# Even attention of a two-block network: a step's four scores in two banks, steps in pairs, masks first, one group copied by VectorE

## The reference

```python
z = h @ w_in
q_a, c_kv, q_i, k_i, w_i, q_b, k_b, v_b = jnp.split(z, ...)
o_a = dsa_attention(...)     # 8 heads; each query attends to the 64 keys that an index score selects
o_b = diff_attention(...)    # 4 heads, each a difference of two softmaxes: p[:, :, 0] - lam * p[:, :, 1]
return jnp.concatenate([o_a, o_b], axis=-1) @ w_out
```

## Time and profile before

| what | value |
|---|---|
| median of 3 runs | 1346.38 us (1346.29 to 1346.5) |
| the profiled execution: its own time | 1346.09 us |
| its span in the trace | 1344.2 us |
| PE busy | 99% of the span |
| DVE, ACT, POOL busy | 72%, 55%, 9% |
| mean granted clock of TensorE | 0.999 of full |
| the even attention, first score to first product of the output projection | 788.61 to 816.57 us |

### The profile page before, as it was taken

How to read it: one execution, slowest core, us unless ns; L and a number is a source line. 1 busy time by engine, 2 the same in 40 slices (tenths; PEclk the granted TensorE clock), 3 DMA queues, 4 the chain that set the end, 5 groups by cost and what they waited for, 6 DMA issues and landing times.

```text
span 1344.2 us, 19217 instructions
## 1 busy us (share of the span) xinstructions
PE 1334.3 (99%) x7365; PEld 1121.7 (83%) x7365; DVE 974.3 (72%) x1502; ACT 740.2 (55%) x1155; POOL 125.3 (9%) x114
## 2 busy tenths in 40 slices
PE   9999999999999999999999999999999999999998
PEld 6888888888888888888888777888888878888886
DVE  7566878777664767877778687886667887786665
ACT  6564555554545754555445676754445675654443
POOL 1000011111000000311111002220000010400000
PEclk9999999999999999999999999999999999999999
DMA  9743545555455334656655524357765524355552
GB/s 375 246 153 129 187 158 193 187 195 192 173 219 186 127 126 160 228 200 231 202 189 201 170 95 151 117 216 227 216 204 193 182 79 173 119 206 193 191 191 88
DMA packets 37673, 244.32 MB, mean 182 GB/s; under 512 B 4656, under 2 KB 5312, under 8 KB 10192
## 3 DMA queue, kind: packets, MB, share of 16 engines
q1 hardware_dynamic: 33568, 228.08, 47.9%
q0 software_dynamic: 3728, 14.82, 3.9%
q10 hardware_dynamic: 288, 0.21, 0.1%
HBM read 241.13 MB, written 1.97 MB: 181 GB/s over the span
## 4 chain that ended last, share of the span: by engine, by line
PE 97%; DVE 1%; ACT 1%; DMA 0%; issue 0%; POOL 0%; ACTq 0%; DVEq 0%
PE ps L1217 19%; PE ps L1155 17%; PE ps L1161 16%; PE ps L1164 16%; PE ps L1224 10%; PE ps L1323 3%; PE ps L1418 2%; PE ps L1449 2%; PE ps L1400 1%; PE ps L2034 1%; PE ps L1265 1%; PE ps L1259 1%; PE ps L1262 1%; PE ps L1577 1%; PE ps L2044 1%; PE ps L1578 1%
## 5 line engine op out<-in xcount | busy, mean ns | idle before, releaser
L2736 DVE TENSOR_TENSOR wlo<-raw,whi 128x1024 fp32r<-128x1024 f32 (+2 forms) x423 | 510.4, 1217 | 264.2 <-ACT whi L2151 263.1
L2151 ACT CAST whi<-raw 128x1024 fp32r<-128x1024 f32 (+1 forms) x431 | 444.6, 1041 | 332.9 <-PE ps L1224 188.5
L1217 PE MATMUL ps<-act,whi 128*128 128x512 f32 x1120 | 266.4, 390 | 0.0
L1217 PEld LDWEIGHTS ps<-act,whi 128*128 128x128 f32 x1120 | 208.4, 188 | 42.2
L1155 PE MATMUL ps<-whi,mhi 128*128 128x512 f32 (+2 forms) x688 | 235.7, 392 | 0.3 <-DVE mlo L2760 0.3
L1161 PE MATMUL ps<-wlo,mhi 128*128 128x512 f32 (+2 forms) x688 | 231.1, 385 | 0.0
L1164 PE MATMUL ps<-whi,mlo 128*128 128x512 f32 (+2 forms) x688 | 231.0, 385 | 0.0
L1164 PEld LDWEIGHTS ps<-whi,mlo 128*128 128x128 f32 x688 | 129.2, 188 | 26.4
L1161 PEld LDWEIGHTS ps<-wlo,mhi 128*128 128x128 f32 x688 | 129.2, 188 | 26.1 <-DVE wlo L2736 0.5
L1224 PEld LDWEIGHTS ps<-act,wlo 128*128 128x128 f32 x1120 | 143.6, 191 | 5.5
L1155 PEld LDWEIGHTS ps<-whi,mhi 128*128 128x128 f32 x688 | 125.9, 188 | 24.1 <-issue 2.4
(11 more groups left out here) (334 smaller groups left out, 1516.3 us busy)
## 6 DMA issues: line engine op xcount, KB each, us to landing
raw<-in_weights SPq DMA_DIRECT2D x210, 1024.0 KB, 4.8
gain_b<-in_norm_g POOLq DMA_DIRECT2D x6, 512.0 KB, 4.0
raw<-in_weights SPq DMA_DIRECT2D x5, 512.0 KB, 5.8
region<-in_b_gate POOLq DMA_DIRECT2D x2, 1024.0 KB, 8.6
o_nat<-in_mem_turned POOLq DMA_DIRECT2D x2, 1024.0 KB, 7.2
region<-band POOLq DMA_DIRECT2D x8, 256.0 KB, 5.0
region<-band POOLq DMA_DIRECT2D x8, 192.0 KB, 5.9
x<-in_x SPq DMA_DIRECT2D x1, 1024.0 KB, 11.6
```

Source lines behind the costliest of these rows:

```text
L1217: nc.tensor.matmul(ps[:, bank0 + f, :], of(whi, h)[:, k, f * P:f * P + P], act2[:, kx].rearrange("p i n -> p (i n)"), start=kx == 0, stop= ...
L2151: nc.scalar.copy(whi[:, m % HL, 0:w], raw[:, n % RAW, h * w:h * w + w]).then_inc(hi_done, 1)
L2736: nc.vector.tensor_tensor(wlo[:, m % HL, 0:w], raw[:, n % RAW, h * w:h * w + w], whi[:, m % HL, 0:w].bitcast(F32), ALU.subtract).then_inc( ...
```

## The change

- The four scores of a step now share two banks: head a in one, head b in the other, qt 0 in columns 0 to 127, qt 1 in columns 128 to 383 (`step_banks`). Even steps use banks 0 and 1; odd ones 6 and 2 (steps 1, 3), then 7 and 3 (steps 5, 7).
- `scores(s)` waits until DVE has taken all of step `s - 2`, and steps are issued in pairs (0, 1), (2, 3), (4, 5), (6, 7).
- The mask of steps 4 to 7 is one product of 384 columns per bank, two a step in place of four, and stands ahead of the scores (`masks`), which then add to it.
- DVE takes a score only when both scores of its bank are done.
- The fourth turned group is copied by DVE, behind the bias of step 1, in place of ACT.
- The outputs of the selecting attention gather in banks 6 and 2, which the difference attention used before; two groups turned for the output projection go to banks 7 and 3. PE waits for both of DVE's outputs (`diff_taken`) before the values of steps 4 and 6.

```diff
-                plan.group((k[0], l) + k[1:], "dve" if k[0] == "qk2" and k[1] in (0, 3, 4) else "act")
+                plan.group((k[0], l) + k[1:], "dve" if k[0] == "qk2" and k[1] in (0, 3, 4) or k == ("qkb", 3) else "act")
...
-            return lambda qt: ((7, 3)[i // 4], SEQ * (i // 2 % 2) + P * qt)
+            return lambda qt: ((6, 2)[i // 4], SEQ * (i // 2 % 2) + P * qt)
...
+        def step_banks(s):
+
+            return (0, 1) if s % 2 == 0 else (6, 2) if s < 4 else (7, 3)
+
...
-                wide_banks = (6, 2) if d["pair"] < 5 else (7, 3) if d["pair"] < 7 else (3, 6)
-                return ps[:, (wide_banks if d["qt"] else (0, 1))[u % 2], 0:d["w"]]
+                return ps[:, step_banks(d["pair"])[u % 2], P * d["qt"]:P * d["qt"] + d["w"]]
...
-                return (6, 2)[key[2] - 2]
+                return (7, 3)[key[2] - 2]
...
+                    def masks(s):
+
+                        if s >= 6:
+                            pe.wait_ge(at_t, u0 + 4 * (s - 1))
+                        for bank in step_banks(s):
+                            nc.tensor.matmul(ps[:, bank, 0:3 * P], ident_b[:], sel[:], start=True, stop=False)
+
                     def scores(s):
 
-                        fours = [(u0 + 4 * s + j, us[4 * s + j]) for j in range(4)]
-                        for qt in range(TT):
-                            pair = fours[2 * qt:2 * qt + 2]
-
-                            pe.wait_ge(at_t, u0 + 4 * s - (0 if qt or not s else 2))
-                            mms = []
-                            for u, d in pair:
-                                (_, _, q, k), = d["parts"]
-                                mms.append(nc.tensor.matmul(scores_of(u, d), q, k, start=True, stop=d["sel"] is None))
-                            if pair[0][1]["joint"]:
-                                for mm in mms:
-                                    mm.then_inc(at_s, 1)
-                        if not fours[0][1]["joint"]:
-                            for u, d in fours:
-                                nc.tensor.matmul(scores_of(u, d), ident_b[:], d["sel"], start=False, stop=True).then_inc(at_s, 1)
+                        if s >= 2:
+                            pe.wait_ge(at_t, u0 + 4 * (s - 1))
+                        for j in range(4 * s, 4 * s + 4):
+                            u, d = u0 + j, us[j]
+                            (_, _, q, k), = d["parts"]
+                            nc.tensor.matmul(scores_of(u, d), q, k, start=d["sel"] is None, stop=d["sel"] is None or d["qt"] == 1).then_inc(at_s, 1)
...
                     scores(0)
+                    scores(1)
                     in2_half(last, 0)
                     groups_at(99)
-                    scores(1)
                     in2_half(last, 1)
-                    taken("qkb", 3)
+                    pe.wait_ge(grp_dve, plan.by_number[plan.groups["qkb", l, 3]][2])
                     scores(2)
+                    scores(3)
                     both_of(turn, 0)
                     in2_half(last, 2)
-                    scores(3)
                     both_of(turn, 1)
                     in2_half(last, 3)
                     pe.wait_ge(sel_ready, TT)
+                    pe.wait_ge(at_t, u0 + 12)
+                    masks(4)
+                    both_of(turn, 2)
+
+                    pe.wait_ge(ev_act, evs_act2(l, "in2", order[-1]))
+                    masks(5)
                     scores(4)
-                    both_of(turn, 2)
-
-                    pe.wait_ge(ev_act, evs_act2(l, "in2", order[-1]))
                     scores(5)
+                    both_of(values, 0)
+                    both_of(values, 1)
                     both_of(turn, 3)
-                    for s in range(4):
-                        both_of(values, s)
+                    both_of(values, 2)
+                    masks(6)
+                    masks(7)
+                    both_of(values, 3)
+                    both_of(turn, 4)
                     scores(6)
-                    both_of(turn, 4)
-                    pe.wait_ge(diff_taken, TT * (l // 2) + 1)
                     scores(7)
                     both_of(turn, 5)
+                    pe.wait_ge(diff_taken, TT * (l // 2) + 1)
                     both_of(values, 4)
                     both_of(turn, 6)
                     both_of(values, 5)
                     both_of(turn, 7)
+                    pe.wait_ge(diff_taken, TT * (l // 2) + 2)
                     both_of(values, 6)
...
-                        if s == 0:
-                            takes_at(99)
...
-                    dve.wait_ge(at_s, u + 1)
+                    dve.wait_ge(at_s, u + 1 if d["pair"] is None else u0 + 4 * d["pair"] + 3 + i % 2)
...
+                        if s == 1:
+                            key = ("qkb", l, 3)
+                            group_ready(dve, key)
+                            nc.vector.tensor_copy(blocks(qT, 6), group_bank(key)).then_inc(grp_dve, 1)
```

More of the change, by code:

```diff
@@ L1869, in _ @@
                     pe.wait_ge(sel_ready, TT)
-                    scores(4)
+                    pe.wait_ge(at_t, u0 + 12)
+                    masks(4)
                     both_of(turn, 2)
                     pe.wait_ge(ev_act, evs_act2(l, "in2", order[-1]))
+                    masks(5)
+                    scores(4)
                     scores(5)
+                    both_of(values, 0)
+                    both_of(values, 1)
                     both_of(turn, 3)
-                    for s in range(4):
-                        both_of(values, s)
+                    both_of(values, 2)
[3 more added lines that the diff above has]
+                    both_of(turn, 4)
                     scores(6)
-                    both_of(turn, 4)
-                    pe.wait_ge(diff_taken, TT * (l // 2) + 1)
                     scores(7)
                     both_of(turn, 5)
+                    pe.wait_ge(diff_taken, TT * (l // 2) + 1)
                     both_of(values, 4)
@@ L2520, in take_dsa @@
                         act.wait_ge(at_o, first_unit["even", l] + 4 * HB + 8 * (g + 1))
-                        nc.scalar.copy(dsa_heads_at(g), ps[:, (7, 3)[g], :]).then_inc(dsa_out, 1)
+                        nc.scalar.copy(dsa_heads_at(g), ps[:, (6, 2)[g], :]).then_inc(dsa_out, 1)
                     def dsa_high(g):
```

## The result

The changed kernel takes 1348.29 us (median of 22 runs, 1348.0 to 1349.93), the kernel before 1346.32 (median of 22 runs beside them). The ratio is 1.0014, with a 95% interval of 1.0008 to 1.002: 1.97 us slower, less than the 0.2% that the forecast counted as a change. The profiled execution took 1348.48 us (span 1346.6).

A forecast was written before the change was run, and what follows sets the result against it. In the even layers' attention stage it took the chain of waits through PE, DVE and ACT as the bound. Profiled 1346.09 us plus 2.1 is 1348.2; with the median 0.29 above that execution, 1348.5 us, range 1346.0 to 1349.8.

The forecast's parts named there:

- pair of steps on PE: Scores of two steps issued together on PE: 1.52 us, with 0.86 for a single step and 0.66 for one following.
- first score product to bias: From a step's first score product on PE to DVE's bias start, now after the third product: 1.03 us (0.97 to 1.18).
- bias 2 later by: Start of DVE's bias work on step 2: 0.14 us later (0.08 to 0.29), though its scores start 0.37 earlier.
- ACT's end to PE's masks: Hand-over from the end of ACT's evacuation to PE's masks of step 5: 0.20 us (0.04 to 0.25).
- bias 4 later by: Start of DVE's bias work on step 4, with its scores behind the evacuation wait: 2.1 us late (1.8 to 2.5).
- nothing makes it up behind bias 4: After DVE's bias on step 4, the links keep their order on DVE and ACT, so the 2.1 us goes through whole.
- ACT's gap: Sign in the changed profile: DVE and ACT with a gap of 2 us or more around 800 to 802.
- the last turn: Sign of being wrong: the stage's last turns on PE come less late than DVE's bias work on step 4.
- PE as the bound: Rival: waits for ACT and DVE cost nothing, merged and interrupted steps save 1.9 us, giving 1344.4 us; chance 0.08.
- ACT's lighter queue: Rival: without the group's copy ACT starts step 2 1.2 us sooner; shift 0.9, time 1347.3 us; chance 0.07.
- The clock: Rival: PE's 1.5 us stand drops its clock from 2.4 to 1.2 GHz; shift 3.4, 1349.8 us or more; chance 0.07.
- the upper end: Rival: paired steps no faster than single ones and every bound at its top; 2.5 + 0.2, 1349.1 us and above; chance 0.08.

The follow-up runs named there:

- e5: The kernel before, with the third turn and the wait for the evacuation of the last projection moved ahead of step 4's scores: 1347.75 us, ratio 1.0012.
- e1: The changed kernel, with step 4's scores issued right behind their masks, ahead of the wait for the evacuation: 1347.24 us, ratio 1.0008.
- f3: e1 with PE's old order behind step 5, steps 6 and 7 single again: 1346.28 us, ratio 1.0.
- e6: f3 with step 4's scores put back behind the wait for the evacuation: 1348.43 us, ratio 1.0016.
- e2: The changed kernel, with ACT's evacuation of the last projection moved ahead of step 3's exponents: 1346.79 us, ratio 1.0004.
- e3: The changed kernel, with the fourth turned group copied by ACT again instead of DVE: 1347.92 us, ratio 1.0012.
- f6: f5's early part, with steps 6 and 7 before the values of 2 and 3, and DVE's first-attention outputs behind step 7's bias: 1350.55 us, ratio 1.0027.
- f5: e1 with the copy on ACT, fourth group turned before the projection's first quarter, steps 2 and 3 after it, 6 and 7 single: 1346.54 us, ratio 1.0.

## Why the prediction was right

The forecast, 1348.5 us and a stage 2.1 us longer by a moved wait, held: 1348.29, 1.79 longer. Its steps, by the two traces:

| term | predicted | measured |
|---|---|---|
| pair of steps on PE | 1.52 | 1.51 |
| masks of one step | 0.33 | 0.33 |
| first score product to bias | 1.03 (0.97 to 1.18) | 0.96, 0.95 (steps 2, 4) |
| bias 2 later by | 0.14 (0.08 to 0.29) | 0.04 |
| evacuation later by | 0.14 | 0.06 |
| ACT's end to PE's masks | 0.20 (0.04 to 0.25) | 0.06 |
| masks of step 5 and the switch | 0.38 | 0.43 |
| bias 4 later by | 2.1 (1.8 to 2.5) | 1.87 |
| stage longer by | 2.1 | 1.79 |

*The mechanism* is shown by experiment, from both sides. Putting the wait ahead of step 4 in the kernel before costs 1.38 (e5), taking it away gives 1.15 in the changed kernel (e1) and 2.37 in f3's order (e6 against f3), and having ACT reach the evacuation sooner removes PE's stand (e2). What the wait costs by itself thus depends on the order behind it.

*The sizes* were 0.2 high up to bias 4 and 0.3 at the end. Three terms came out lower than forecast: the hand-over from the third product to DVE, the shift of bias 2 that hangs on it (0.04, below its own bound), and the hand-over from ACT to PE, 0.05 of issue in the chain, where I had taken a row of 0.25 for the nearest. That row was no hand-over: in the kernel before, PE's own product ahead of the first score ran until 788.49.

```profile
787.47 1.02 PE L1788 MATMUL ps<-work,region 128*128 128x512 f32 x2
```

Two other readings were off and cancelled: the four transposes take 0.35 us of PE (791.87 to 792.22), not 0.44, their length in the chain, and the quarter behind them 1.50 (to 793.72), not 1.43. So the switch on the way into a step was 0.18 (0.53 less 0.35), not 0.09.

*That nothing makes it up behind bias 4* was nearly so. Bias 6 is 1.70 late, not 1.87: the reciprocal of the outputs follows the first one after 0.12 us (807.26 to 807.38) where it took 0.25 before (805.07 to 805.32), as it does in e6 (0.25).

```profile
805.32 0.18 DVE L3460 RECIPROCAL rden<-den 128x4 f32<-128x4 f32 x1
```

The program lets this reciprocal wait for PE's values (`at_o`), so at this link the old chain went through PE. That the change's order behind step 5 softens a late step 4 by 0.3 (e6) was not in the prediction. Nor was that the same order costs 0.9 as soon as step 4 is early (e1 against f3): I had said that the links stand in the same order on DVE and ACT, which is true, but a turn moved on PE held ACT.

*Signs and luck.* Two of the signs that the prediction named came out a little on the other side: ACT's gap is 1.78 us and not 2, and the last turn, of step 7, is 1.80 late (from 812.58 to 814.70, each behind its own first score) where bias 4 is 1.87 late; the prediction had called a lesser delay of the last turns a sign of being wrong.

```profile
812.58 1.04 PE L1418 MATMUL ps<-cst,work 128*128 128x128 f32 x6
```

That the output projection starts at 818.68, as foretold, is luck: the stage began 0.32 later and lasted 0.3 less than the forecast had it. So is part of the time's fit, since 0.25 of the 1.97 us are DVE's pause behind the stage (e3), which was not in the sum.

*The rivals.* PE as the bound is out: PE saved its 0.21 us per pair and the stage grew. The Trainium skill, "TensorEngine Tiling (Array Packing)", Key Properties, has the drain at a mode change; the 1.51 us of a pair against 2 x 0.86 agrees with it, and it moved no end. ACT's lighter queue did not free the banks sooner: bias 2 hung on scores that began at 793.72 (DVE idle 0.36, released by L1848), and e3 finds the copy's place worth nothing for bias 2 to 6. The clock did not fall in the changed kernel: 1.00 in the window with the stand of 1.32 us. f6 shows this mechanism, behind a stand of 2.62 us. Paired steps took 1.51, not 1.72, so the upper end is out too.

*What stays open.* Both of DVE's pauses, inside bias 6 and behind the stage, come and go with the copy on DVE (e3), but what makes DVE pause is not shown. What the program lets it wait for had come earlier: the first instruction of bias 6 waits for the same scores as the third, and POOL had ended 0.29 us before. That the change's order gives 0.3 back by filling PE's stand of 1.40 us is read from the traces of e6 and the changed kernel; no run was made for it.

## What to carry to other kernels

A kernel that is "99% PE" can hold stages bound by other engines; there, time saved on PE by pairing and packing is worth nothing by itself, and a wait that is moved one step forward in PE's in-order queue holds all that stands behind it (1.4 to 2.4 us here). Before regrouping work by bank, ask of each wait which work behind it doesn't need it, and leave that work ahead. After a fix, look at the next link: in e1 and f5 a transpose that had been moved behind larger products held ScalarE by 0.4 and 1.0 us and ate much of the gain.

## What was not expected of the hardware

A stand of 2.62 us on PE in f6 was followed by half the granted clock (0.50, the 1.2 GHz level) over the 4 us window from 818 to 822, though PE was busy for all of it. Windows of 1 us narrow it: 0.70 from 816 to 817, in which PE had no product, 0.50 from 817 to 823, 0.89 from 823 to 824 and 1.00 from there. The stands of 1.30 and 1.32 us in the changed kernel left it at 1.00, and so did those of 1.31 and 1.40 us in e6. The Trainium skill, "TensorE: Matmul & The Clock Gate", Part 1, has such a rule, an idle stretch that halves the clock; f6 agrees with it in kind. Part of f6's loss is this and not the wait: the eight transposes and twelve value products behind the stand took 3.38 us, from 817.01 to 820.39, against 2.22 in the changed kernel, which has the 0.32 us wait for DVE in it.

The other surprise is DVE's pause: the copy that the change puts into DVE's program was followed by a pause of 0.25 us at a place some 316 us further on, in six profiles of six (e3).
